# Output projections in two token passes, the next stage's first groups by token half, and modulation matmuls in bursts of four

## What is computed

```
def modulation(cvec, w, b):                       # 9 vectors of 1024 for each layer, latents and context apart
    m = silu(cvec) @ w + b
def pre(x, mod_j, gain):
    return rmsnorm(x, gain) * (1 + scale) + shift
def ffn_sublayer(x, mod_j, g_pre, g_post, w_in, w_out):
    h = pre(x, mod_j, g_pre)
    g, u = split(h @ w_in)                        # w_in 1024 x 5632
    return x + 0.5 * mod_j[2] * rmsnorm((silu(g) * u) @ w_out, g_post)
```

## Time and profile before

| | us |
|---|---|
| median of three runs | 3012.33 |
| span of the profiled execution (first to last instruction) | 3013.7 |
| PE busy (matmul) | 2740.7 |
| VectorE, ScalarE, GpSimd busy | 681.4, 520.2, 190.8 |
| FFN-in matmuls (L576) | 1069.8 |
| mean granted TensorE clock | 0.961 |

### The profile page before, as it was taken

The page is one execution under the profiler, slowest core; times in us unless marked ns, Lnnn a source line. Parts: engine busy times, 40 slices in busy tenths (PEclk is TensorE's granted clock), DMA queues, the critical chain, the costliest instruction groups (busy, mean ns, idle before and its releaser), DMA issues.

```text
span 3013.7 us, 27300 instructions
## 1 busy us (share of the span) xinstructions
PE 2740.7 (91%) x10207; PEld 1513.3 (50%) x10207; DVE 681.4 (23%) x1393; ACT 520.2 (17%) x816; POOL 190.8 (6%) x260
## 2 busy tenths in 40 slices
PE   4999999899968888888899999899999979968998
PEld 1444433244457767783344433334443435736887
DVE  1100000255146555661300000120000030162001
ACT  1000000222142233212100000110000020173111
POOL 1000011000011121110000001100001000010000
PEclk7999999999979999999999999999999989998999
DMA  6222466222200000002122256422226303102452
GB/s 228 80 74 78 117 200 191 91 81 72 68 4 1 0 0 0 1 1 77 56 83 70 86 164 197 138 70 70 84 80 182 106 30 98 56 0 98 152 167 72
DMA packets 243277, 257.75 MB, mean 86 GB/s; under 512 B 6297, under 2 KB 223891, under 8 KB 243091
## 3 DMA queue, kind: packets, MB, share of 16 engines
q1 hardware_dynamic: 222483, 181.43, 19.6%
q0 software_dynamic: 20736, 75.51, 7.9%
HBM read 255.87 MB, written 1.05 MB: 85 GB/s over the span
## 4 chain that ended last, share of the span: by engine, by line
PE 83%; DVE 6%; issue 5%; ACT 4%; DMA 1%; DVEq 1%; POOL 0%; SPq 0%; ACTq 0%; POOLq 0%
PE bank L576 35%; PE bank L537 31%; PE bank L511 3%; PE bank L728 2%; PE bank L726 2%; PE bank L809 2%; PE bank L711 2%; DVE hs L1335 1%; PE bank L660 1%; ACT L888 1%; DMA mring<-in_w_mod 1%; DVE hs L1483 1%; PE bank L747 1%; PE bank L831 1%; DVE hs L1156 1%
## 5 line engine op out<-in xcount | busy, mean ns | idle before, releaser
L576 PE MATMUL bank<-hs,ring 128*128 128x512 f32 (+1 forms) x2816 | 1069.8, 542 | 23.6 <-DVE hs L1161 23.6
L576 PEld LDWEIGHTS bank<-hs,ring 128*128 128x128 f32 x2816 | 536.9, 191 | 553.5 <-issue 520.5
L537 PE MATMUL bank<-big,ring 128*128 128x512 f32 (+1 forms) x1664 | 651.9, 542 | 9.1 <-POOL big L449 5.5
L537 PEld LDWEIGHTS bank<-big,ring 128*128 128x128 f32 x1664 | 307.6, 191 | 296.0 <-issue 272.5
L537 PE MATMUL bank<-hs,ring 128*128 128x512 f32 (+2 forms) x784 | 319.0, 570 | 12.9 <-DVE hs L1161 12.7
L1173 DVE TENSOR_TENSOR big<-bank,room 128x512 f32 (+1 forms) x88 | 55.0, 625 | 993.8 <-PE bank L576 993.8
L537 PEld LDWEIGHTS bank<-hs,ring 128*128 128x128 f32 (+1 forms) x784 | 151.3, 194 | 180.5 <-issue 169.2
L917 ACT ACT_TABLE_LOAD x44 | 56.5, 1283 | 747.3 <-PE bank L576 747.3
L402 POOL DMA_DIRECT2D mring<-in_w_mod x144 | 76.2, 529 | 1473.2 <-PE bank L511 1470.4
L1091 ACT ACTIVATE hs<-bank 128x512 f32 (+1 forms) x48 | 25.2, 526 | 724.4 <-PE bank L537 724.4
L711 PE MATMUL bank<-mring,hs 128*128 128x128 f32 x768 | 106.0, 284 | 19.4 <-DVE hs L1335 19.4
(11 more groups left out here) (202 smaller groups left out, 1774.6 us busy)
## 6 DMA issues: line engine op xcount, KB each, us to landing
ring<-in_ffn_w_in SPq DMA_DIRECT2D x88, 1024.0 KB, 5.0
mring<-in_w_mod POOLq DMA_DIRECT2D x144, 512.0 KB, 4.0
ring<-in_ffn_w_out SPq DMA_DIRECT2D x32, 1408.0 KB, 7.1
ring<-in_gdn_w_in SPq DMA_DIRECT2D x16, 1024.0 KB, 5.6
ring<-in_diff_w_in SPq DMA_DIRECT2D x12, 1024.0 KB, 5.1
ring<-in_gdn_w_out SPq DMA_DIRECT2D x4, 1024.0 KB, 5.2
ring<-in_diff_w_out SPq DMA_DIRECT2D x4, 1024.0 KB, 5.2
cst<-in_consts SPq DMA_DIRECT2D x1, 1600.0 KB, 7.1
```

The source lines that it names most:

```text
L537: last = mm(bank[0:rows, r % 4, 0:cols], w[:, k, :], rhs(k), start=(k == 0), stop=(k == n_k - 1))
L576: last = mm(bank[:, (g0 + 2 * v + jj) % 4, 0:TOK - c0], w[:, k, jj * P:(jj + 1) * P], hs[:, k, c0:TOK], start=(k == 0), stop=(k == KC - 1))
```

## The change

- Output projections of stages 0 to 3 run in two passes: all 8 groups for the context columns, then all 8 for the latent ones (256 columns each). In the FFNs chunks 4 to 7 come first in the second pass (their weights are still in the ring), and four weight units are loaded again.
- The root of a norm is taken on [128, 2] columns (tokens on partitions): the ones-matmul has the sums of squares stationary, ScalarE Sqrt, VectorE reciprocal, and a matmul with the identity spreads it over a bank. Post-scale and pre-scale/shift move to ScalarE; VectorE works on two chunks at once.
- The context half's chain stands between the latent output groups. The next stage's first four groups (`first_four`) are split: four context halves, then four latent halves; the latent half's chain stands between them.
- Stage 0's pre-norm stands between the first modulation units.
- Modulation units go out in bursts of four (`mod_four`) after a group of FFN-in; `mod_unit` and GpSimd's loads are not touched.
- Stage 4 projects keys before queries.

```diff
-MOD_FIRST = 16
-MOD_GATE = 8
-MOD_INSIDE = {0: 48, 2: 48, 3: 24}
+MOD_FIRST = 2
+MOD_PAIRS = {0: {0: 2, "loop": 3, 9: 7, 10: 8}, 2: {"loop": 9, 9: 13, 10: 14}, 3: {0: 15, 9: 16, 10: 17}}
...
+            def post_sum(e):
...
+                for t in range(2):
+                    last = mm(bank[:, 6, t:t + 1], ssq[:, at + t * P:at + (t + 1) * P], ones[:, 0:1], start=True, stop=True)
+            def pre_sum(p):
+                pe.wait_ge(S["x_summed"], (p + 1) * 3)
...
+            def post_spread(e):
+                pe.wait_ge(S["post_recip"], e + 1)
+                for t in range(2):
+                    last = mm(bank[:, 6, LAT + t * P:LAT + (t + 1) * P], rt[:, 2 + t:3 + t].to_broadcast([P, P]), ident,
+                              start=True, stop=True)
...
+            between_mods = {1: lambda: pre_sum(0), 2: lambda: pre_spread(0), 5: lambda: pre_sum(1), 6: lambda: pre_spread(1)}
...
+                def mod_four(i, half):
+                    for k in range(4):
+                        mod_unit(i, 4 * half + k)
+
+                def first_four(mod=None):
...
+                    for q in range(4):
+                        if q % 2 == 0:
+                            unit_wait(u0 + q // 2, u0 + q // 2)
+                        pe.wait_ge(S["acc_freed"], g0 + q + 1)
+                        if n and q == 1:
+                            post_spread(e)
+                        half(q, side[1], 1)      # context; in q 0 after k 3: post_sum, in q 3 after k 1: pre_sum
+                    if n:
+                        pre_spread(p)
+                    for q in range(4):
+                        half(q, side[0], 0).then_inc(S["acc_done"], 1)
+                        if mod is not None and q in (0, 2):
+                            mod_four(mod, q // 2)
...
+                    def whole_vector(i):
+                        return ((0, lambda: mod_four(i, 0)), (2, lambda: mod_four(i, 1)), (3, lambda: mod_turn(i)))
+                    with pe.Fori(0, FC // 4 - 1) as it:
+                        if "loop" in vecs:
+                            i = it * 1 + vecs["loop"]
+                            pair(it * 2 + 1, 2, after=((3, lambda: mod_four(i, 0)),))
+                            pair(it * 2 + 2, 4, after=((1, lambda: mod_four(i, 1)), (3, lambda: mod_turn(i))))
...
+                    for i in (9, 10):
+                        pair(i, 2 * i, after=whole_vector(vecs[i]) if i in vecs else ())
...
+                if n < 4:
+                    e, p = post_event(n, 1), pre_event(n + 1, 1)
+                    chain = {0: lambda: post_sum(e), 1: lambda: post_spread(e), 4: lambda: pre_sum(p), 5: lambda: pre_spread(p)}
+                    for q in range(KC):
+                        out_group(0, q, 1, side[1])
+                    for q in range(KC):
+                        out_group(1, q, 0, side[0])
+                        chain.get(q, nothing)()
...
+            def post_rooted(e):                   # ScalarE
+                act.wait_ge(S["post_sum"], e + 1)
+                fn(rt[:, 0:2], bank[:, 6, 0:2], ACT.Sqrt, bias=eps_col[:, 0:1], scale=1.0 / D).then_inc(S["post_rooted"], 1)
+            def affine(n, v, ks):
...
+                for k in ks:
+                    act.wait_ge(S["h_scaled"], p * 4 + k // 2 + 1)
+                    fn(hs[:, k, side[v]], hs[:, k, side[v]], ACT.Identity, bias=modv[:, m, v, k:k + 1],
+                       scale=pre_scale[:, n, v, k:k + 1]).then_inc(S["h_ready"], 1)
...
+            def update(e, v):                     # VectorE
+                dve.wait_ge(S["post_root"], e + 1)
+                r = bank[:, 6, LAT:TOK].unsqueeze(1).to_broadcast([P, 2, LAT])
+                for jx in range(5):
+                    if jx < 4:
+                        y = hs[:, 2 * jx:2 * jx + 2, side[v]]
+                        v_.tensor_tensor(y, y, r, ALU.mult).then_inc(S["y_scaled"], 1)
+                    if jx:
...
+                        v_.tensor_tensor(x_, x_, y, ALU.add).then_inc(S["x_updated"], 1)
+            def x_sums(p, js):
+                for jx in js:
+                    dve.wait_ge(S["x_squared"], p * 4 + jx + 1)
...
+                    v_.tensor_tensor(ssx, ssx, xsq[jx % 2], ALU.add).then_inc(S["x_summed"], 1)
```

More of the change, by code:

```diff
@@ L225, in hybrid_backbone @@
         ssq = carve(TOK)
+        ssx = carve(2, LAT)
+        xsq = [sg[:, b, :].rearrange("p (a t) -> p a t", a=2) for b in range(2)]
         carve = Carver(room, ROOM)
@@ L544, in _, with pre_spread, nothing @@
+            def pre_spread(p):
+                pe.wait_ge(S["pre_recip"], p + 1)
+                for t in range(2):
+                    last = mm(bank[:, 7, LAT + t * P:LAT + (t + 1) * P], rt[:, 6 + t:7 + t].to_broadcast([P, P]), ident,
+                              start=True, stop=True)
+                last.then_inc(S["pre_root"], 1)
+            def nothing():
+                pass
             pe.wait_ge(S["cond_ready"], 1)
             pe.wait_ge(S["x_updated"], KC)
-            with pe.Fori(0, MOD_FIRST // KC) as i:
+            between_mods = {1: lambda: pre_sum(0), 2: lambda: pre_spread(0), 5: lambda: pre_sum(1), 6: lambda: pre_spread(1)}
@@ L547, in _ @@
+            for i in range(MOD_FIRST):
                 for k in range(KC):
                     mod_unit(i, k)
+                    between_mods.get(i * KC + k, nothing)()
                 mod_turn(i)
             for n, (kind, l, j) in enumerate(SUBS):
[L552 to L557, removed]
@@ L616, in _ @@
[L616 to L631, removed]
+                                for q, what in after:
+                                    if q == 2 * v + jj:
+                                        what()
@@ new lines, in _, with in_unit @@
+                if kind != "ffn":
+                    first_four()
+                if kind == "gdn":
+                    def in_unit(i, r):
+                        unit_wait(u0 + i * 4 + r, u0 + r)
+                        for jj in range(2):
+                            q = 2 * r + jj
+                            group(g0 + i * 8 + q, g0 + q, slot(u0 + r, KC, 256)[:, :, jj * P:(jj + 1) * P],
+                                  lambda k: hs[:, k, :], starts=(jj == 0))
+                    for r in (2, 3):
+                        in_unit(0, r)
+                    with pe.Fori(1, 4) as it:
+                        for r in range(4):
+                            in_unit(it, r)
@@ L908, in _ @@
+            nc.scalar.preload_act_table(ACT.Sqrt)
+            for v in (1, 0):
+                p = pre_event(0, v)
+                x_squares(p, v, range(4))
+                pre_rooted(p)
+            for v in (1, 0):
+                affine(0, v, range(KC))
+            for n, (kind, l, j) in enumerate(SUBS):
+                g0 = group0[n]
+                width = LAT if n > 4 else TOK
                 if kind == "ffn":
@@ new lines, in _ @@
+                scales_post(n)
+                if n < 5:
+                    scales_pre(n + 1)
+                if n < 4:
+                    e, p = post_event(n, 1), pre_event(n + 1, 1)
+                    chain = {1: lambda: update(e, 1), 2: lambda: x_sums(p, (1,)), 3: lambda: x_sums(p, (2, 3)),
+                             4: lambda: pre_recip(p), 5: lambda: h_scale(p, 1)}
+                    for q in range(1, KC):
+                        add_square(q, 1)
+                    post_recip(e)
+                    for q in range(1, KC):
+                        add_square(q, 0)
+                        if q in chain:
+                            chain[q]()
+                else:
+                    for q in range(1, KC):
+                        add_square(q, 0)
```

377 lines of the change are left out of this document (227 added, 150 removed).

## The result

The changed kernel takes 3059.65 us (median of 4 runs, 3057.48 to 3062.53), the kernel before 3012.7 beside it: ratio 1.016, 95% interval 1.0145 to 1.0174. It is slower, by 47 us of the medians; 3063 was predicted. The profiled execution has a span of 3058.7 us, 45 more than before.

The account below looks back on a forecast made before the run. TensorE (PE), busy 91% of 3013.7 us, and its idle time were taken as the bound. 3013.7 - 103 - 4 - 4 - 14 + 4 + 105 + 67 = 3064.7, or 3063 us against the runs' median; range 2990 to 3105.

Parts of the forecast that it names:

- The wait: Modulation bursts in FFN-in: each fourth unit waits for its load, 32 x 3.28 = +105 us (89 to 115).
- The clock: Behind each of 32 bursts PE's granted clock falls to half, 2.1 us each: +67 us (48 to 96).
- Rival (B): Bursts wait for their fourth load but the clock stays up: 2996 us, faster; chance 0.14.
- The boundaries: Four stage boundaries: norm chains hide beside split output and projection halves, each keeping 4.7 us: -103 us.
- narrower matmuls: Output passes of 256 columns, with what a boundary between groups may add: +4 us (0 to 10).
- Rival (D): Boundaries don't close: VectorE's longer chain stops PE, 10 us lost at each of four: 3103 us; chance 0.08.
- The start: Stage 0's pre-norm between the first modulation units lets FFN-in begin earlier: -14 us (-8 to -17).
- Stage 4 to 5: Boundary with latents only, its chain not hidden; 18.2 us before, about 13.9 after: -4 us (0 to -6).
- the tail: Final post-norm: two table loads go, root and update passes shorten: -4 us (-2 to -5).
- (A): The main case, all terms as summed: 3063 us, own range 3022 to 3103; chance 0.73.
- Rival (C): Bursts don't wait: the fourth load lands in time, no clock price: 2860 us; chance 0.05.
- theory L: Expectation for e8: where code lies, set at build, makes the DeltaNet heads slow: again 543 us.

Follow-up runs that it names:

- e9: The changed kernel unaltered, run again on the third chip: 3073.6 us.
- e11: The changed kernel with four filler matmuls on constants before the fourth unit of every burst, on the third chip: 2999.7 us.
- e5: The changed kernel with stage 0's pre-norm put back behind the 16 modulation units instead of between them: 3090.8 us.
- e8: The changed kernel unaltered, run again on the second chip: 3076.6 us.
- mended gate: The changed kernel with units reporting at their last matmul and the count starting at 4, so all four slots fill: 2879.65 us, again 2877.2 us.
- e7: The kernel before with modulation bursts of four in FFN-in and the mended gate, old boundaries kept: 2976.5 us.
- e3: The changed kernel with four filler matmuls on constants between the third and fourth unit of every burst: 3001.4 us.
- e4: The kernel before with only its modulation units moved into FFN-in in bursts of four, old gate and boundaries kept: 3173.6 us.
- e6: The changed kernel with two filler matmuls, not four, before the fourth unit of every burst: 3012.55 us over 10 runs.
- e2: The changed kernel with its gate as it is, but the modulation units spread after FFN-in groups instead of in bursts: 2925.3 us.
- e12: The changed kernel with modulation units spread and each vector's last unit one group earlier, ahead of the transposes: 2901.4 us.
- e1: The changed kernel with the mended gate, first measurement: 2879.65 us.
- e10: The changed kernel with the mended gate, run again on the third chip: 2877.2 us.

## Why the prediction was right, step by step

- **The wait: right, +105 predicted, +90 measured.** 32 x 5.76 - 94.7 by the first profile. The mechanism, the number of bursts and the place are as predicted; the fourth unit came 4.94 us after the first, not 5.5. The burst above leaves 136.38 - 132.65 = 3.7 us from issue to use, where I had counted 4.3. By the Trainium skill ("DMA: Bandwidth & Descriptors", the anatomy of one DMA) a load of 512 KB takes, as an estimate from its fit, 3.2 us. This case's trace has more, the 3.7 us just named. With e9's 5.98 us a burst it is +97.
- **The clock: right, +67 predicted, 66 measured** by e9 against e11, and about 61 in the first profile (FFN-in of the three stages less 3 x 302.4 us of projections, the bursts and the start's and boundaries' losses). The clock fell behind 31 of 32 bursts in the first profile and behind all 32 in e9, at 2.07 us a burst. The Trainium skill ("TensorE: Matmul & The Clock Gate", HAM oscillation) tells of a loop in which DMA waits let the clock fall at every tile. The trace agrees but for that one burst. The estimate of 0.83 us a wait that I worked out from its figures is not this kernel's, and the measurement decides. Rival (B), the clock holds, is out.
- **The boundaries: right in mechanism, mis-sized with their narrower matmuls: -103 + 4 predicted, -92 measured.** FFN-out takes 154.2 us for 151.2 (3.0 more, not 2.0), and the four split groups lose 4.7, not 3.5; so three boundaries give 21.4, 22.2 and 21.4 and the last 27.3. The one wait of the latent chain is 1.49 us where 1.3 was worked out. Rival (D) is out.
- **The start: right, -14 predicted**, 14.2 by e5 against e8. **Stage 4 to 5** gives 2.5 for 4 (15.7 us against 18.2), **the tail** 3.0 for 4.
- **Missed: the heads of stage 1, +7.6 us**, code that the change does not touch.

Sum by the profiles: -92 - 15 - 2.5 - 3 + 90 + 61 + 8 = +47, measured +45 by the spans; predicted +51. So the closeness of the total is in part luck, errors that cancel: the gains net of the narrower matmuls were put 9 us too large (121 for 112), which with the missed heads makes 17, and the losses 21 too large (172 for 151). The own range of (A), 3022 to 3103, has no working: the bounds of its terms, added at their ends, give 3009 to 3133. Rival (C), no wait, was the wrong forecast for this gate and the right one for the mended gate: 2860 said, 2880 measured.

**A version that beats both.** The changed kernel with the mended gate: 2879.7 and 2877.2 us, 4.4 and 4.5% below the kernel before. By e7, 97 of these 134 us are boundaries, start and tail, and 37 the units, of which four loaded ones in a row cost 1.84 us instead of 2.96.

## What to carry to other kernels

A ring of n slots whose refill waits for the *start* of unit u-n+1 holds only n-1 units ahead. Here, spread out, nothing waited for it; n units together made every burst wait for a load. Before bunching work, count what is in the ring when the bunch begins, and release a slot by its last reader. A wait in PE's own queue can be paid twice, once as time and once as clock: here 3.9 and 2.1 us a burst.

## What the runs showed of the hardware that was not expected

The heads of stage 1, the same source in all kernels, take 520.2 to 523.6 us in the kernel before, e3, e4, e6, e7 and e11, and 526.9 to 530.3 in the first profile after, e2, e5, e8, e9 and e12, repeatably for one program (529.7, 530.3, 528.2), as e8's theory L had it. The mended kernel lies between and less repeatably: 524.3 in e1, 527.4 in e10. The list of PE's waits in the first profile after, and the instruction queue's traffic over the heads (871 to 1401 us), have:

```profile
PE bank L797 <- issue: 10.9, 4, 2.9
q8 instruction: 31, 0.51, 0.4%
```

In the kernel before no such wait stands in the list, and the instruction queue moved 0.21 MB there; e7 and e11 have 0.20 MB and no such wait either, e9 and e12 0.51 MB and 10.0 and 10.7 us of it, e1 and e10 0.51 MB and 9.7 and 9.9 us. So these waits go with the instructions that a program fetches inside this loop and not with the run. They explain the heads' length only roughly, since e1, with 9.7 us of them, is less than 1 us longer than e6, with none. That the place of the loop in the program sets them is likely, but only argued.
